# Gathers of a paged latent cache spread over the tiles in which their memory is free, and pooling sums moved ahead of the rotations

## The chip, the cores and the metric

One Trainium2 chip, of which the kernel uses one core. The metric is the device time of one execution in microseconds (us). The kernel before took 2307.67 us, the median of 3 runs (2307.08 to 2310.55).

## The reference, cut to what matters

One layer of a decoder runs over two kinds of input: a prompt of 1024 tokens, and 8 decode sequences with one new token each and 8192 cached tokens each. All arithmetic is float32. The parts the change touches are these.

```python
# pooling: trailing means over 2, 4, 8, 16 positions minus the token, one window per channel group
win = end[..., ch] - cs[:, P + 1 - w:P + 1 - w + S, ch]
diffs.append(win / cnt - bf[:, P:, ch])
# latents and the shared rotary key
ckv = rms_norm(c_kv_raw, g_kv_a);  kpe = apply_rope(k_pe_raw, cos, sin)
# decode attention: for each of 8 sequences, over its 64 pages of 128 cached tokens
k = mla_keys(cache_ckv[phys], cache_kpe[phys], w_uk, g_kn)     # keys from the latent, RMS-normed per head
s = einsum('bqhd,bkhd->bhqk', q, k) * scale                    # then softmax over 8192 tokens
acc = acc * alpha + einsum('bhqk,bkc->bhqc', p, ckv_blk)       # weighted latents
```

`cache_ckv` holds 256 floats for each cached token and `cache_kpe` 32. `page_table` says which physical page is which.

## The kernel before, in words

The program has four stages: input projection with the per-head projections behind it (about 0 to 248 us), prompt attention (to 418 us), decode attention over the cache (419 to about 1400 us), and the output projection with the gated MLP. Every engine has its own instruction stream, written out by hand, and waits on semaphores. The order of the text of a stream is its order of execution.

**Decode attention** (`cache_and_merge`). The 8 sequences (b = 0 to 7) follow one another. Each has 64 tiles of 128 tokens, handled as 32 pairs (n = 0 to 31), and 8 chunks of 8 tiles. For each pair TensorE transposes two tiles of the following pair into PSUM (`turn`, L1676), then makes keys of this pair with 12 matmuls (`keys`, L1700). ScalarE copies the transposed latents to SBUF (`hi`, L1872), VectorE makes their low part (L2063), ScalarE squares the keys (L1972), and VectorE takes the scores (L2176, semaphore `scored`) and the sums of squares (L2178, semaphore `summed`, one increment per tile). `summed` therefore counts tiles that are done. Every fourth pair also handles the rotary keys of a chunk (L1708, L1716). Ahead of pair 18 of sequence b+1, that is once its tile 36 is the next, TensorE makes the softmax-weighted latents of sequence b (`weigh`, L1728, 130 matmuls, semaphore `weighted`). From then on the latents of sequence b are dead. VectorE and ScalarE also build the key weights of the following sequence in pairs 17 to 25 of sequences 0 to 6 (L2030, L2038, L1977).

**Gathers** (`gather`, L1401). The latents come by indirect DMA, issued from GpSimd's stream. One chunk is two transfers: 128 KB of rotary keys into a ring of 12 slots, and 1 MB of latents into `lat[par][n]`, where par is the sequence's parity. So there are 16 transfers per sequence and two sequences' memory. Chunk 0 of sequence 0 is gathered at the start of the prompt attention. When the cache stage begins, GpSimd issues chunks 1 to 7 of sequence 0 without a wait, then `paced(1)`. After that, for each b, it runs `tail(b)` (norms and scaled scores of sequence b), waits for `weighted` of b, and issues `paced(b + 2)`. `paced(b)` issues chunk 0 at once and chunk n when `summed` has reached 7n tiles of sequence b-1. As `weighted` comes at tile 36, the conditions 7, 14, 21, 28 and 35 are already met for b of 2 and more: chunks 0 to 5 go out back to back, chunk 6 at tile 42, chunk 7 at tile 49. For b = 1 nothing has to be weighed first, so the eight chunks go out at tiles 0, 7, 14 and so on.

**Input projection** (`inputs_and_heads`). Nine tiles are projected by TensorE; the order is the decode tokens first and then the eight prompt tiles. GpSimd's stream has two duties for each tile n. `rotate(n)` (L550 to L555) rotates the shared key of tile n once VectorE has copied it (`kpe_out`, L503); its result (`roped`) lets VectorE copy the next. `average(n - 2)` (L575 to L590) makes the pooling sums of prompt tile n-2 once ScalarE has stored that tile (`u_kept`, L316), and it also contains the subtraction for the tile before (`subtract`, L596, semaphore `averaged`). The loop does `rotate(n)`, then `average(n - 2)`. After the loop come `average(7)`, `subtract(7)`, and then the rotations of the query heads (`heads.gpsimd`, L1035 to L1040, semaphore `rotated`). In the head stage behind it, ScalarE's copy of the values of tile 1 (L868) waits until `averaged` has reached 8, since its destination lies in the memory around the pooling input; TensorE's transposes (L783) need the PSUM banks that ScalarE empties, and those of the query heads need `rotated`.

Of the kernel before, what the change touches and what calls it, by code (L numbers as in the profile page):

```python
# [124 lines left out]
def inputs_and_heads(nc, io, keep):  # L125
# [9 lines left out]
    with ExitStack() as stack:  # L135
# [397 lines left out]
        def _(pool):  # L533
# [11 lines left out]
            def rotate(n):  # L545
                pool.wait_ge(kpe_out, n + 1)
                a, b_ = kpe_raw[:, 0:HR], kpe_raw[:, HR:DR]
                i = ORDER[n]
                cos, sin = keep.cos[:, i, :], keep.sin[:, i, :]
                nc.gpsimd.tensor_tensor(rot[:, 0, :], a, cos, ALU.mult)  # L550
                nc.gpsimd.tensor_tensor(rot[:, 1, :], b_, sin, ALU.mult)
                nc.gpsimd.tensor_tensor(rot[:, 2, :], b_, cos, ALU.mult)
                step(nc.gpsimd.tensor_tensor(rot[:, 3, :], a, sin, ALU.mult))
                step(nc.gpsimd.tensor_tensor(keep.kpe[:, i, 0:HR], rot[:, 0, :], rot[:, 1, :], ALU.subtract))
                nc.gpsimd.tensor_tensor(keep.kpe[:, i, HR:DR], rot[:, 2, :], rot[:, 3, :], ALU.add).then_inc(roped, 1)  # L555
# [14 lines left out]
            def average(i):  # L570

                c0, add = HIST + i * P, ALU.add
                uT = keep.uT
                pool.wait_ge(u_kept, i + 2)
                step(nc.gpsimd.tensor_tensor(sum2[:], uT[:, :, c0 - 14:c0 + P], uT[:, :, c0 - 15:c0 + P - 1], add))  # L575
                if i >= 1:
                    subtract(i - 1)
                step(nc.gpsimd.tensor_tensor(sum4[:], sum2[:, 1:4, 2:142], sum2[:, 1:4, 0:140], add))
                step(nc.gpsimd.tensor_tensor(sum8, sum4[:, 1:3, 4:140], sum4[:, 1:3, 0:136], add))
                step(nc.gpsimd.tensor_tensor(sum16[:], sum8[:, 1, 8:136], sum8[:, 1, 0:128], add))  # L580
                if i >= 1:
                    pool.wait_ge(averaged, i)
                sums = (sum2[:, 0, 14:142], sum4[:, 0, 12:140], sum8[:, 0, 8:136], sum16[:])
                for g, src in enumerate(sums):
                    last = nc.gpsimd.tensor_scalar(mean[:, g, :], src, 1.0 / WINDOWS[g], 1.0, ALU.mult, ALU.mult)
                step(last)
                if i == 0:
                    pool.wait_ge(counts_in, 16)
                    for g, src in enumerate(sums):
                        last = nc.gpsimd.tensor_tensor(mean[:, g, 0:16], src[:, 0:16], keep.counts[:, g, :], ALU.mult)  # L590
                    step(last)

            def subtract(i):

                tile = keep.uT[:, :, HIST + i * P:HIST + (i + 1) * P]
                nc.gpsimd.tensor_tensor(tile, mean, tile, ALU.subtract).then_inc(averaged, 1)  # L596

            pool.wait_ge(w_lo_done, DC)
            for n in range(2, NT):
                rotate(n)  # L600
                average(n - 2)
            average(PT - 1)
            subtract(PT - 1)
            pool.wait_ge(pages_in, 16 * 12)
# [771 lines left out]
CHUNKS = PAST // CHUNK  # L1376
TILES = PAST // P
# [25 lines left out]

def cache_and_merge(nc, io, keep):

    PACE = 7
    with ExitStack() as stack:
        c = Ctx(nc, stack, "ca")
        slot_in = keep.slot_in
# [77 lines left out]
        keyed, squared, summed, scored = c.sem("keyed"), c.sem("squared"), c.sem("summed"), c.sem("scored")  # L1487
# [112 lines left out]
        @block.gpsimd  # L1600
        def _(pool):
            def chunk_sums(i):

                n = width(i)
                pool.wait_ge(mix_squared, i + 1)
                step(nc.gpsimd.tensor_tensor(msq[:, :, 0:2, 0:n], msq[:, :, 0:2, 0:n], msq[:, :, 2:4, 0:n], ALU.add))
                nc.gpsimd.tensor_tensor(msq[:, :, 0, 0:n], msq[:, :, 0, 0:n], msq[:, :, 1, 0:n], ALU.add)\
                  .then_inc(chunks_added, 1)

            def tail(b):  # L1610

                par = b % 2
                if b >= 1:
                    pool.wait_ge(shifted, b)
                for n, (a, z) in enumerate(PARTS if b == NB - 1 else ((0, TILES),)):
                    if n == 1:
                        chunk_sums(0)
                    pool.wait_ge(summed, b * TILES + z)
                    pool.wait_ge(pe_summed, b * CHUNKS + z // 8)
                    step(nc.gpsimd.tensor_tensor(mean[:, a:z], ss[:, par, a:z], kss[:, par, a:z].unsqueeze(2)  # L1620
                                                 .to_broadcast([P, z - a, NH]), ALU.add))
                    nc.gpsimd.tensor_scalar(mean[:, a:z], mean[:, a:z], 1.0 / DH, EPS, ALU.mult, ALU.add)\
                      .then_inc(averaged, 1)
                    pool.wait_ge(scored, b * TILES + z)
                    pool.wait_ge(pe_out, b * CHUNKS + z // 8)
                    step(nc.gpsimd.tensor_tensor(raw[:, par, a:z], raw[:, par, a:z], rot[:, par, a:z], ALU.add))
                    pool.wait_ge(averaged, b + 1 + n)
                    pool.wait_ge(guessed, b + 1 + n)
                    step(newton_rsqrt(nc.gpsimd, step, guess[:, a:z], mean[:, a:z], guess[:, a:z], tmp[:, a:z]))
                    step(nc.gpsimd.tensor_tensor(raw[:, par, a:z], raw[:, par, a:z], guess[:, a:z], ALU.mult))  # L1630

                nc.gpsimd.tensor_copy(raw[:, par, TILES, :], keep.s_new[:, b, :]).then_inc(complete, 1)
                if b == NB - 1:
                    chunk_sums(1)

                pool.wait_ge(reduced, b + 1)
                nc.gpsimd.tensor_tensor(raw[:, par], raw[:, par], top_all[:].unsqueeze(1)
                                        .to_broadcast([P, TILES + 1, NH]), ALU.subtract).then_inc(shifted, 1)

            step = Steps(pool, pool_step)  # L1640

            def paced(b):

                for n in range(CHUNKS):
                    if n >= 1:
                        pool.wait_ge(summed, (b - 1) * TILES + PACE * n)
                    gather(nc, io, keep, b, (n,))

            gather(nc, io, keep, 0, range(1, CHUNKS))
            pool.wait_ge(keep.mixed_stored, 16 * (1 + NH // 2))  # L1650
            paced(1)
            for b in range(NB):
                tail(b)
                if b + 2 < NB:
                    pool.wait_ge(weighted, b + 1)
                    paced(b + 2)
            for i in range(2, NT):
                chunk_sums(i)
            down.gpsimd(pool)
# [1172 lines left out]
```

## Time and profile before

| | |
|---|---|
| median of 3 runs | 2307.67 us |
| profiled execution, own time | 2308.59 us |
| its span (first to last instruction) | 2306.8 us |
| TensorE busy | 2208.0 us, 96% of the span |
| VectorE busy | 1420.0 us, 62% |
| ScalarE busy | 957.0 us, 41% |
| GpSimd busy | 362.3 us, 16% |
| software DMA queue (GpSimd's) | 84.92 MB, 10.1% of the engines' time |

A view by windows gives for each stretch of the execution how long every engine was busy (in the order PE, PEld, DVE, ACT, POOL, with the count of instructions), the granted TensorE clock (1.00 is 2.4 GHz, 0.50 is 1.2 GHz), the share of the 16 DMA engines' time that was used, and GB/s. The chain of waits goes back from the last instruction to what released it. In a timeline, the bracket at the end of a row says how long the engine had been idle before the instruction and what ended that.

### The profile page before, as it was taken

How to read it: one execution, taken by the hardware profiler on the slowest of the kernel's cores; microseconds unless marked ns; L12 is line 12 of the kernel's file. 1: busy time of each engine (PE TensorE's matmuls, PEld its weight loads, DVE VectorE, ACT ScalarE, POOL GpSimd, SP SyncE). 2: the span in 40 equal slices, each digit the busy share in tenths (PEclk: the TensorE clock that was granted, in tenths of full speed). 3: DMA queues.
4: the chain of work that ended last, by engine and by line, in shares of the span. 5: the costliest groups of instructions: out<-in, count | busy, mean ns of one | idle time of the engine just before them, and what ended most of it. 6: DMA issues, size and time to landing. Idle time of an engine off the chain costs nothing.

```text
span 2306.8 us, 34165 instructions
## 1 busy us (share of the span) xinstructions
PE 2208.0 (96%) x12929; PEld 1856.8 (80%) x12929; DVE 1420.0 (62%) x2682; ACT 957.0 (41%) x1829; POOL 362.3 (16%) x501
## 2 busy tenths in 40 slices
PE   8989899799999999999898999999999999999999
PEld 7977566688687877778686877879999999988776
DVE  4346676476565666667565766666767676754345
ACT  4445565355454545445454554321211111133334
POOL 2454111311212212031212103200000000000000
PEclk9999999999999999999999999999999999999999
DMA  5300100520312203040404013321111111143443
GB/s 166 63 18 1 58 16 19 201 101 26 133 37 86 84 30 136 6 165 6 165 5 172 12 42 127 116 79 46 45 45 45 45 45 45 36 148 118 165 170 132
DMA packets 94627, 182.17 MB, mean 79 GB/s; under 512 B 9264, under 2 KB 64384, under 8 KB 86127
## 3 DMA queue, kind: packets, MB, share of 16 engines
q1 hardware_dynamic: 78781, 95.48, 12.7%
q0 software_dynamic: 15712, 84.92, 10.1%
q8 instruction: 82, 1.34, 0.2%
q14 instruction: 52, 0.43, 0.1%
HBM read 166.34 MB, written 14.35 MB: 78 GB/s over the span
## 4 chain that ended last, share of the span: by engine, by line
PE 77%; issue 2%; DVE 1%; ACT 1%; another core or an unknown queue 1%; DMA 0%; POOL 0%; SPq 0%; DVEq 0%; ACTq 0%; POOLq 0%
PE ca_banks L1700 31%; PE ca_banks L2334 21%; PE ca_banks L2607 10%; PE ca_banks L1676 5%; PE ca_banks L1781 4%; PE ca_banks L1728 3%; PE ca_banks L1716 1%; PE ca_banks L1708 1%; PE ca_banks L2583 0%; PE ca_banks L1812 0%; DVE ca_room L2445 0%; DMA ca_x<-in_x_prompt 0%; DVE ca_down_lo L2647 0%; PE ca_banks L1765 0%
## 5 line engine op out<-in xcount | busy, mean ns | idle before, releaser
L1700 PE MATMUL ca_banks<-cache_w_hi,ca_hi 128*128 128x512 f32 x1024 | 431.1, 421 | 46.0 <-DVE ca_cells L2176 24.1
L1972 ACT ACTIVATE ca_banks<-ca_banks 128x512 f32<-128x512 f32 x512 | 297.9, 582 | 390.6 <-PE ca_banks L1700 247.1
L1700 PE MATMUL ca_banks<-cache_w_lo,ca_hi 128*128 128x512 f32 x1024 | 406.1, 397 | 0.0
L1700 PE MATMUL ca_banks<-cache_w_hi,ca_lo 128*128 128x512 f32 x1024 | 405.8, 396 | 0.0
L2178 DVE TENSOR_REDUCE ca_cells<-ca_banks 128x8 f32<-128x512 f32 x512 | 348.3, 680 | 0.0
L1700 PEld LDWEIGHTS ca_banks<-cache_w_hi,ca_hi 128*128 128x128 f32 x1024 | 195.8, 191 | 83.9 <-issue 47.5
L2063 DVE TENSOR_TENSOR ca_lo<-ca_banks,ca_hi 128x512 fp32r<-128x512 f32 x256 | 175.7, 686 | 103.9 <-ACT ca_hi L1872 82.7
L2176 DVE TENSOR_TENSOR ca_cells<-ca_banks,attn_coef 128x8 f32<-128x8 f32 x512 | 84.5, 165 | 243.3 <-ACT ca_banks L1972 228.7
L1700 PEld LDWEIGHTS ca_banks<-cache_w_hi,ca_lo 128*128 128x128 f32 x1024 | 195.5, 191 | 46.0
L1700 PEld LDWEIGHTS ca_banks<-cache_w_lo,ca_hi 128*128 128x128 f32 x1024 | 196.7, 192 | 32.8
L1872 ACT ACTIVATE ca_hi<-ca_banks 128x512 fp32r<-128x512 f32 x256 | 152.6, 596 | 92.5 <-PE ca_banks L1676 79.6
L2445 DVE RECIPROCAL ca_room<-ca_room 128x1032 f32<-128x1032 f32 x22 | 145.3, 6603 | 0.8
L2607 PE MATMUL ca_banks<-ca_down_hi,ca_g_hi 128*128 128x512 f32 x352 | 113.9, 405 | 2.1 <-DVE ca_gT L2448 1.9
L2379 ACT ACTIVATE ca_room<-ca_banks 128x1032 f32<-128x1032 f32 x22 | 22.8, 1035 | 219.9 <-PE ca_banks L2334 219.9
L2334 PE MATMUL ca_banks<-mlp_h_hi,ca_gate_hi 128*128 128x344 f32 x528 | 113.4, 321 | 0.6 <-DVE mlp_h_lo L2141 0.6
L2647 DVE TENSOR_TENSOR ca_down_lo<-ca_down_raw,ca_down_hi 128x1024 fp32r<-128x1024 f32 x44 | 53.9, 1225 | 97.1 <-ACT ca_down_hi L2638 97.1
L2334 PE MATMUL ca_banks<-mlp_h_lo,ca_gate_hi 128*128 128x344 f32 x528 | 113.3, 320 | 0.0
L2334 PE MATMUL ca_banks<-mlp_h_hi,ca_gate_lo 128*128 128x344 f32 x528 | 112.7, 319 | 0.0
L1401 POOL DMA_INDIRECT cache_kpe<-in_cache_kpe,attn_index x64 | 61.3, 958 | 326.1 <-DVE ca_cells L2178 152.1
L2334 PE MATMUL ca_banks<-mlp_h_hi,ca_up_hi 128*128 128x344 f32 x528 | 112.2, 321 | 0.0
L2334 PE MATMUL ca_banks<-mlp_h_lo,ca_up_hi 128*128 128x344 f32 x528 | 111.6, 319 | 0.0
L2334 PE MATMUL ca_banks<-mlp_h_hi,ca_up_lo 128*128 128x344 f32 x528 | 111.5, 319 | 0.0
(408 smaller groups left out, 4086.6 us busy)
## 6 DMA issues: line engine op xcount, KB each, us to landing
ca_down_raw<-in_w_down SPq DMA_DIRECT2D x44, 512.0 KB, 3.3
keep_w_uv<-in_w_gate SPq DMA_DIRECT2D x22, 512.0 KB, 3.8
ca_up_raw<-in_w_up SPq DMA_DIRECT2D x22, 512.0 KB, 3.6
keep_ctx<-in_w_down SPq DMA_DIRECT2D x22, 512.0 KB, 3.4
late_room<-in_x_prompt SPq DMA_DIRECT2D x8, 512.0 KB, 3.9
ca_m<-mixed_scratch SPq DMA_DIRECT2D x8, 512.0 KB, 4.3
ca_w_raw<-in_w_o SPq DMA_DIRECT2D x16, 256.0 KB, 2.5
ca_x<-in_x_prompt SPq DMA_DIRECT2D x8, 512.0 KB
```

Of the source, the lines that this page charges most:

```text
L1676: last = nc.tensor.transpose(TT[:, n % 2, (2 * t + ck) * P:(2 * t + ck + 1) * P], src, keep.ident[:])
L1700: last = nc.tensor.matmul(KK[:, t, :], x[:, n % 2, t, ck, :], w[:, par, ck, :], start=(m == 0), stop=(m == 5))
L1728: last = nc.tensor.matmul(CT[q * 32:q * 32 + NH, 0:RK], probs[:, t, :], v, start=(t < 4), stop=(t >= TILES - 3))
L1781: last = nc.tensor.matmul(OUT[0:n, a, g, :], h[:, k, 0:n], w[:, k, g * 512:(g + 1) * 512], start=(k == 4 * a and q == 0), stop=(k == 4 * a ...
L1872: nc.scalar.activation(hi[:, n % 2], TT[:, n % 2, :].rearrange("p (t c k) -> p t c k", t=2, c=2), ACT.Copy).then_inc(hi_done, 1)
L1972: nc.scalar.activation(SQ[:, t, :], KK[:, t, :], ACT.Square).then_inc(squared, 1)
L2063: nc.vector.tensor_tensor(lo[:, n % 2], TT[:, n % 2, :].rearrange("p (t c k) -> p t c k", t=2, c=2), hi[:, n % 2].bitcast(F32), ALU.subtra ...
L2176: nc.vector.tensor_tensor(raw[:, par, 2 * n + t, :], KK[:, t, :].rearrange("p (h d) -> p h d", d=DN)[:, :, 0], keep.coef[:, b, :], ALU.mul ...
L2178: nc.vector.tensor_reduce(ss[:, par, 2 * n + t, :], SQ[:, t, :].rearrange("p (h d) -> p h d", d=DN), AX.X, ALU.add).then_inc(summed, 1)
L2334: ins = nc.tensor.matmul(GU[kind][:, j, :], w[kind][:, k, :], h[:, k, j * F3:(j + 1) * F3], start=(k == 0 and n == 0), stop=(k == DC - 1 a ...
L2445: link(nc.vector.reciprocal(sig, sig))
L2607: last = nc.tensor.matmul(self.OUT[t][:, h, :], g[b][:, t * P:(t + 1) * P], w[b][:, h * 512:(h + 1) * 512], start=(f == 0 and k == 0), sto ...
```

## The change

Four edits. The loop of the input projection does `average(n - 2)` before `rotate(n)`. `paced(b)` issues chunk n, chunk 0 included, when `summed` has reached 36 + 7n // 2 tiles of sequence b-1, which is 36, 39, 43, 46, 50, 53, 57 and 60. Chunks 1 and 2 of sequence 0 go out at once and chunk n from 3 to 7 when `summed` has reached 8(n - 2), which is 8, 16, 24, 32 and 40. `paced(1)`, behind them, follows the same rule of 36 to 60. The number and size of the transfers, their destinations and all arithmetic are the same.

```diff
@@ inputs_and_heads, gpsimd
             pool.wait_ge(w_lo_done, DC)
             for n in range(2, NT):
+                average(n - 2)
                 rotate(n)
-                average(n - 2)
             average(PT - 1)
             subtract(PT - 1)
@@ cache_and_merge
-    PACE = 7
+    START, PACE = 36, 7
@@ cache_and_merge, gpsimd
                 for n in range(CHUNKS):
-                    if n >= 1:
-                        pool.wait_ge(summed, (b - 1) * TILES + PACE * n)
+                    pool.wait_ge(summed, (b - 1) * TILES + START + PACE * n // 2)
                     gather(nc, io, keep, b, (n,))
 
-            gather(nc, io, keep, 0, range(1, CHUNKS))
+            gather(nc, io, keep, 0, (1, 2))
+            for n in range(3, CHUNKS):
+                pool.wait_ge(summed, TILES // CHUNKS * (n - 2))
+                gather(nc, io, keep, 0, (n,))
             pool.wait_ge(keep.mixed_stored, 16 * (1 + NH // 2))
             paced(1)
```

## Rows read from the trace of the kernel before

**Rows 1.** The page: its first line, and the chain of waits by engine.

```profile
span 2306.8 us, 34165 instructions
...
PE 77%; issue 2%; DVE 1%; ACT 1%; another core or an unknown queue 1%; DMA 0%; POOL 0%; SPq 0%; DVEq 0%; ACTq 0%; POOLq 0%
```

**Rows 2.** Chain of waits in sequence 1 (start us, us, what).

```profile
621.00 4.21 another core or an unknown queue
```

**Rows 3.** Windows: stretch and its us, engines' busy us, PEclk, DMA share, GB/s.

```profile
430.99:447.10 16.11, 5.46 (x20) 4.23 (x19) 4.04 (x10) 2.87 (x6) 6.89 (x8) 0.68 0.94 386
457.15:460.58 3.43, 3.43 (x19) 2.86 (x18) 2.80 (x8) 1.69 (x4) 1.28 (x2) 1.00 0.00 0
620.49:631.55 11.06, 5.99 (x21) 4.41 (x20) 4.92 (x12) 3.02 (x6) 6.03 (x7) 0.69 1.00 404
743.91:754.77 10.86, 5.74 (x21) 4.20 (x20) 4.64 (x12) 3.00 (x6) 5.79 (x7) 0.69 1.01 406
867.28:877.87 10.59, 5.54 (x21) 4.05 (x20) 4.43 (x12) 3.00 (x6) 5.54 (x7) 0.84 1.01 408
990.23:1000.81 10.58, 5.49 (x22) 4.04 (x21) 4.39 (x11) 3.00 (x6) 5.55 (x7) 0.84 1.01 403
1113.27:1125.99 12.72, 6.17 (x21) 4.85 (x20) 5.19 (x12) 3.09 (x6) 5.93 (x7) 0.73 0.93 368
1238.35:1252.37 14.02, 6.10 (x21) 4.83 (x20) 5.10 (x12) 3.00 (x6) 5.95 (x7) 0.63 1.00 387
1364.88:1368.55 3.67, 3.67 (x21) 3.14 (x20) 3.47 (x9) 2.52 (x5) 0.00 (x0) 1.00 0.25 76
```

**Rows 4.** GpSimd's timeline: first and last gather of a burst, one paced gather.

```profile
610.90 1.02 POOL L1401 DMA_INDIRECT cache_kpe<-in_cache_kpe,attn_index  x1 [22.45 <-PE ca_banks L1728]
...
625.26 0.95 POOL L1401 DMA_INDIRECT cache_lat_late<-in_cache_ckv,attn_index  x1 [0.30 <-issue]
...
642.09 0.95 POOL L1401 DMA_INDIRECT cache_kpe<-in_cache_kpe,attn_index  x1 [10.16 <-DVE ca_cells L2178]
```

**Rows 5.** Windows of four pairs each in sequence 0: pairs 8 to 11, 20 to 23.

```profile
460.58:474.06 13.48, 13.48 (x72) 11.30 (x71) 9.15 (x22) 7.34 (x15) 2.49 (x3) 1.00 0.29 102
...
501.02:514.63 13.61, 13.61 (x72) 11.32 (x71) 10.63 (x26) 8.29 (x17) 1.89 (x2) 1.00 0.26 88
```

**Rows 6.** A window of the input projection.

```profile
54.00:60.00 6.00, 6.00 (x41) 5.61 (x39) 1.52 (x7) 3.11 (x7) 5.61 (x9) 1.00 0.98 180
```

**Rows 7.** GpSimd's timeline, end of the pooling sums.

```profile
165.50 1.14 POOL L575 TENSOR_TENSOR in_sum<-mid_uT 128x568 f32<-128x568 f32 x1
...
171.98 1.18 POOL L596 TENSOR_TENSOR mid_uT<-late_room,mid_uT 128x512 f32<-128x512 f32 x1
173.12 0.46 POOL L1035 TENSOR_TENSOR keep_ctx<-keep_ctx,late_cos 128x128 f32<-128x128 f32 x1
```

**Rows 8.** ScalarE's timeline, same stretch.

```profile
144.13 0.60 ACT L316 ACTIVATE mid_uT<-in_tr 128x512 f32<-128x512 f32 x1 [6.10 <-PE in_tr L399]
...
173.19 0.60 ACT L868 ACTIVATE mid_v<-in_tr 128x512 f32<-128x512 f32 x1 [8.58 <-POOL mid_uT L596]
...
176.09 0.20 ACT L856 ACTIVATE hd_log<-hd_mean 128x16 f32<-128x16 f32 x1
```

**Rows 9.** TensorE's timeline, same stretch.

```profile
173.84 1.09 PE L783 MATMUL in_tr<-keep_ident,hd_k_nat 128*96 128x128 f32 x4 [6.17 <-ACT mid_v L868]
175.91 1.91 PE L783 MATMUL in_tr<-keep_ident,keep_ctx 128*96 128x128 f32 x8 [0.98 <-POOL keep_ctx L1040]
```

**Rows 10.** VectorE's timeline: the last step of tile 1's mean.

```profile
173.22 0.39 DVE L963 TENSOR_SCALAR hd_mean<-hd_ss 128x16 f32<-128x16 f32 x1
```

**Rows 11.** GpSimd's timeline of one tile: rotation, then last pooling step.

```profile
95.15 0.22 POOL L550 TENSOR_TENSOR in_rot<-in_kpe_raw,late_cos 128x16 f32<-128x16 f32 x1 [7.77 <-DVE in_kpe_raw L503]
...
101.95 0.30 POOL L585 TENSOR_SCALAR late_room<-in_sum 128x128 f32<-128x128 f32 x1
```

**Rows 12.** ScalarE's timeline of the same tile.

```profile
87.19 0.58 ACT L316 ACTIVATE mid_uT<-in_tr 128x512 f32<-128x512 f32 x1
```

## The prediction, made before the changed kernel was run

> **What bounds the kernel now.** I read the page's chain of waits by engine first: 77% of it is TensorE [rows 1]. So a change counts only where it shortens TensorE's idle time, or lengthens it. The small shares beside it are the interesting ones: "issue" 2% and "another core or an unknown queue" 1% are waits for which the profile has no releaser. Following the chain in order of time through the decode attention, one such piece of 4 to 7 us stands in each of the sequences 0 to 6, as the 4.21 us at 621.00 [rows 2]. Nothing of the program's own ended it.
>
> Next I took the start of each pair's transposes from TensorE's timeline and asked the windows for the pairs in which these pieces lie [rows 3]. Pair 21 of sequence 7 takes 3.67 us, with no gather issued in it (GpSimd 0.00). Pair 21 of sequences 1 to 6 takes 11.06, 10.86, 10.59, 10.58, 12.72 and 14.02 us. In sequence 0 it is pair 3, with 16.11 us against 3.43 us for pair 7 of the same sequence. TensorE was busy for 5.5 to 6.2 us of each, the granted clock averages 0.63 to 0.84 (part of it at 1.2 GHz, after the idle time), and the DMA engines were in use 93 to 101% of the time at 368 to 408 GB/s. The same place in the program costs 7 to 13 us more exactly where a burst of gathers is in flight: in sequences 1 to 6 twelve transfers go out back to back, the first at 610.90 and the last at 625.26 [rows 4], 6.75 MB in all.
>
> In the input stage the same kind of reading finds one more hole: TensorE waits 6.17 us for ScalarE's L868 [rows 9], which had waited 8.58 us for GpSimd's last pooling subtraction [rows 8].
>
> **The change part by part.**
>
> *Gathers paced.* Excess of the seven pairs [rows 3]: 16.11 - 3.43 = 12.68, then minus 3.67 each: 7.39, 7.19, 6.92, 6.91, 9.05 and 10.35; the sum is 60.49 us. This includes the half clock behind each hole. The pairs around them stand at their regular length, so nothing is hidden elsewhere. After the change no two chunks go out closer than 3 tiles, except chunks 1 and 2 of sequence 0. A pair takes 13.48 / 4 = 3.37 us [rows 5], so 3.5 tiles are 5.9 us. A chunk is 1.125 MB, 2.9 us at 404 GB/s: one chunk is landed 3 us before the next is issued. Whether that is sparse enough is answered by gathers that are paced already: seven chunks of sequence 1, 7 tiles apart, go out during sequence 0, and chunk 7 of each later one goes out alone, as at 642.09 [rows 4]. Four pairs that contain one or two of them last 13.48 and 13.61 us [rows 5]. So an isolated chunk costs 0 to 0.13 us. There are 63 chunks behind the first, so 0 to 8 us. I take 0, the value of the first row, since the 13.61 also holds the building of the next weights. Upper bound of the loss from the opening of sequence 0, where four transfers still go back to back: its 12.68 us stay. Lower bound: 0. I take 0: an issue of the burst takes (625.26 - 610.90) / 11 = 1.31 us, so the hole at 621.00 comes after some eight transfers, four chunks, not two.
>
> What queues behind the new waits: on GpSimd, `paced(1)` waits behind chunk 7 of sequence 0, and `tail(b)` behind the last gather. The last gather is now issued at tile 60 (it was tile 49) and takes two issues of 0.95 us [rows 4], about 1.1 tiles with the gaps; `tail` itself waits for tile 64. Cost 0, cover about 3 tiles, 5 us. Who needs the data: chunk n of sequence 0 is issued at tile 8(n - 2) and transposed from tile 8n - 2, 14 tiles or 24 us later; for the other sequences chunk 0 has 26 tiles and chunk 7 has 58. Cost 0. The waits for the ring of rotary keys are met earlier than the new conditions.
>
> *Sums ahead of rotations, at the end.* After the last rotation GpSimd now has one set of sums left, not two. One set takes 171.98 - 165.50 = 6.48 us there [rows 7]; tile 6's own is ready from 144.13 + 0.60 [rows 8] and runs before the rotation. So `averaged` reaches 8 at about 166.7 instead of 173.16, L868 runs 6.5 us earlier and the head rotations start 6.4 us earlier; TensorE's transposes at 173.84 and 175.91 [rows 9] move with them. A smaller wait comes into view: VectorE ends tile 1's mean at 173.61 [rows 10] and ScalarE's logarithm of it ran at 176.09 [rows 8], so that chain gains only 2.5 us. It gates the transposes of the next tile, which come behind a whole projection, and I take that as slack enough. Without the 6 us of idle time the clock should also stay up behind it; I put 0.5 us on that, an estimate. I take 7 us; bounds 0 (the chain of VectorE and ScalarE holds everything) and 8.6 (ScalarE's whole idle time).
>
> *Sums ahead of rotations, in the loop.* A rotation now waits behind a set of sums. For one tile: the input is stored at 87.19 + 0.58 = 87.77 [rows 12], the sums take 102.25 - 96.47 = 5.8 us (the rotation at 95.15 takes 1.3 and the last step ends at 102.25) [rows 11], so they end at 93.6, 1.6 us before the rotation can start. Cost 0 with 1.6 us of cover. With the cover gone VectorE copies the next key late, and TensorE needs that PSUM bank only one tile later. The sums now run beside VectorE's normalisation; some of those small instructions may wait for GpSimd. Bounds -1 to +5 us over seven tiles; I take 0.
>
> *Sum.* 2308.59 - 60.49 - 7 = 2241.1 us for an execution like the profiled one. That one lies 0.92 us over the median of the runs, so 2240.2 us; I write 2240.
>
> **A rule against this.** TensorE's holes coincide with a saturated DMA in [rows 3]. The Trainium skill, page "SBUF — State Buffer", section "Who interferes with whom", says that a DMA never contends with a compute engine and that PE and ACT never wait on anyone. By that rule the transfers do not cause the holes, pacing changes nothing, and the sum would be about 2301. No row shows a hole with the DMA engines idle, so the trace does not agree so far.
>
> **Rivals.**
>
> *The holes are not the burst's.* Their place is always pair 21 in sequences 1 to 6, where the next key weights are made (pairs 17 to 25), and sequence 7, without a hole, makes none. Also, 6 us of fully used DMA in the input stage leave TensorE 6.00 of 6.00 us busy [rows 6]. Then only the pooling part counts: 2307.67 - 7 = 2300.7. Against it: pairs 20 to 23 of sequence 0 make those weights with only single chunks in flight and take 13.61 us for all four [rows 5], and the hole of sequence 0 is at pair 3, where no weights are made. The rule above would do the same here. Chance 6%.
>
> *Part of the hole stays.* If it comes with a certain number of transfers close together, sequence 0's opening can keep its 12.7: 2253. If each of the seven keeps half, 30 us, 2270. For it: the hole starts 10 us after the first issue, well inside the burst, and ends while the burst goes on, so it is not the length of the burst that sets it. Against it: the paced chunks show nothing of it. Chance 12% and 8%.
>
> *Slower: one hole for each stretch of transfers.* Each burst has exactly one hole, though it keeps the DMA full for 17 us. If the hole belongs to the beginning of a stretch that meets a bad moment, there are now 8 stretches a sequence where there were two. At two holes of 6.9 us a sequence, 2 x 6.91 x 7 = 96.7 us come for 60.5: 2307.67 + 36.2 - 7 = 2337. It decides from ten holes on (67.5 / 6.91 = 9.8) in about 56 stretches. Against it: 13 single chunks in the trace without one. Chance 3%.
>
> **How the numbers follow.** All holes gone 71%, opening of sequence 0 kept 12%, halves kept 8%, no effect 6%, slower 3%. The range goes from 2235 (60.5 + 8.6 off the median, and the runs' own spread of 3) to 2266 (opening kept, isolated chunks at 0.13 us each, no gain in pooling: 2307.67 - 47.8 + 8 = 2268). A difference below 0.2%, 4.6 us, can't be told from none. Faster by more 96%; the same 1%; slower 3%.
>
> **What would show it.** Right: no pair in the decode attention over 4 us outside the weighings; seven unattributed pieces gone from the chain; the granted clock at 1.00 from 420 to 1340 us; gathers of later sequences 5 to 7 us apart; L868 about 6.5 us earlier, and TensorE's first matmul of the cache stage at about 412 instead of 419. Wrong: holes at pair 21 with the DMA engines half idle (first rival), shorter holes (second), more than one a sequence (third), or rotations that end later than before in the loop.

## The result, and the profile after

| | before | after |
|---|---|---|
| median | 2308.07 us (4 runs, 2307.08 to 2310.55) | 2243.4 us (4 runs, 2240.52 to 2243.67) |
| profiled execution, span | 2306.8 us | 2241.9 us |
| ratio after / before | | 0.9716, 95% interval 0.9701 to 0.9732 |

That is 64.7 us less; 67.5 was forecast, and 2240. But one of the four chips of the experiments below ran the kernel before in 2248.8 us, and there the pacing brought nothing. So the larger part of this gain depends on the chip, or on its state at the time. The excess of TensorE's time at a burst of gathers is called a hole from here on.

The page after: engines, and the chain of waits by engine.

```profile
PE 2191.6 (98%) x12929; PEld 1845.9 (82%) x12929; DVE 1425.7 (64%) x2682; ACT 955.5 (43%) x1829; POOL 363.4 (16%) x501
PE 79%; DVE 1%; ACT 1%; issue 0%; DMA 0%; POOL 0%; ACTq 0%; DVEq 0%; POOLq 0%
```

"issue" went from 2% to 0% and "another core or an unknown queue" from 1% to nothing [rows 1]. The windows after for the places of [rows 3] (stretch and its us, engines' busy us, PEclk, DMA share, GB/s): pair 3 of sequence 0, pair 21 of sequences 1 and 6, and two neighbouring pairs late in sequence 0.

```profile
424.18:427.61 3.43, 3.43 (x20) 2.86 (x19) 2.79 (x8) 1.69 (x4) 0.00 (x0) 1.00 0.00 0
602.88:606.66 3.78, 3.78 (x22) 3.16 (x20) 3.78 (x11) 1.92 (x4) 0.00 (x0) 1.00 0.85 277
...
1183.72:1187.52 3.80, 3.80 (x21) 3.17 (x20) 3.80 (x11) 1.91 (x4) 0.00 (x0) 1.00 0.83 276
495.13:499.75 4.62, 3.73 (x19) 2.60 (x17) 2.16 (x6) 2.73 (x6) 0.82 (x1) 1.00 0.97 379
499.75:503.89 4.14, 3.86 (x21) 3.16 (x20) 3.36 (x9) 1.91 (x4) 1.57 (x2) 1.00 0.50 195
```

Pair 3 went from 16.11 to 3.43 us, and pair 21 of the six sequences from 10.6 to 14.0 to between 3.75 and 3.80. The last two rows are new: pairs 24 and 25 of sequence 0, whose like (every fourth pair, by the starts of the transposes) take 3.20 and 3.67 us elsewhere, take 4.62 and 4.14. GpSimd's timeline of that place shows why (start us, us, what; two rows of ten).

```profile
483.15 0.94 POOL L1401 DMA_INDIRECT cache_kpe<-in_cache_kpe,attn_index  x1 [11.29 <-DVE ca_cells L2180]
...
495.00 0.94 POOL L1401 DMA_INDIRECT cache_lat_far<-in_cache_ckv,attn_index  x1 [0.30 <-issue]
```

Ten transfers went out back to back. `paced(1)` stands behind chunk 7 of sequence 0, which waits for tile 40. By then its own conditions 36 and 39 are met, and 43 and 46 are met while it catches up.

The cache stage as a whole, first of before, then of after:

```profile
419.25:1396.31 977.06, 930.64 (x5384) 754.23 (x5385) 629.86 (x1500) 495.39 (x940) 202.51 (x206) 0.98 0.22 83
```

```profile
412.43:1331.41 918.98, 916.84 (x5383) 745.41 (x5384) 628.57 (x1500) 493.92 (x940) 200.88 (x206) 1.00 0.27 88
```

It is 58.08 us shorter; the other 6.8 of the span's 64.9 us come before it. The head stage after, by engine:

```profile
166.67 1.18 POOL L596 TENSOR_TENSOR mid_uT<-late_room,mid_uT 128x512 f32<-128x512 f32 x1
167.81 0.64 POOL L1035 TENSOR_TENSOR keep_ctx<-keep_ctx,late_cos 128x128 f32<-128x128 f32 x1
168.41 1.04 POOL L1036 TENSOR_TENSOR keep_ctx<-keep_ctx,late_sin 128x128 f32<-128x128 f32 x1
167.89 0.60 ACT L868 ACTIVATE mid_v<-in_tr 128x512 f32<-128x512 f32 x1 [2.10 <-POOL mid_uT L596]
172.66 0.22 ACT L856 ACTIVATE hd_log<-hd_mean 128x16 f32<-128x16 f32 x1 [2.03 <-DVE hd_mean L963]
168.28 1.05 PE L783 MATMUL in_tr<-keep_ident,hd_k_nat 128*96 128x128 f32 x8 [1.50 <-DVE hd_k_nat L988]
171.42 1.91 PE L783 MATMUL in_tr<-keep_ident,keep_ctx 128*96 128x128 f32 x8 [2.09 <-POOL keep_ctx L1040]
```

ScalarE's L868 waits 2.10 us instead of 8.58 [rows 8], and TensorE's hole of 6.17 us before the key transposes [rows 9] is 1.50 us, ended by VectorE. The query transposes now wait 2.09 us for GpSimd's rotation.

### The profile page after: what moved, and what is told of

It reads as the page before. It is cut to its first block, busy times and chain, and to the rows that moved or that the text cites. A ratio compares the mean times of both kernels' runs of the same rounds, so it can differ in the third digit from the quotient of the medians.

```text
span 2241.9 us, 34172 instructions
## 1 busy us (share of the span) xinstructions
PE 2191.6 (98%) x12929; PEld 1845.9 (82%) x12929; DVE 1425.7 (64%) x2682; ACT 955.5 (43%) x1829; POOL 363.4 (16%) x501
## 4 chain that ended last, share of the span: by engine, by line
PE 79%; DVE 1%; ACT 1%; issue 0%; DMA 0%; POOL 0%; ACTq 0%; DVEq 0%; POOLq 0%
PE ca_banks L1702 31%; PE ca_banks L2336 22%; PE ca_banks L2609 11%; PE ca_banks L1678 5%; PE ca_banks L1783 4%; PE ca_banks L1730 3%; PE ca_banks L1718 1%; PE ca_banks L1710 1%; PE ca_banks L2585 0%; PE ca_banks L1814 0%; DVE ca_room L2447 0%; DVE ca_down_lo L2649 0%; DMA ca_w_raw<-in_w_o 0%; ACT ca_down_hi L2640 0%; PE ca_banks L1767 0%
## 5 line engine op out<-in xcount | busy, mean ns | idle before, releaser
L1702 PE MATMUL ca_banks<-cache_w_hi,ca_hi 128*128 128x512 f32 x1024 | 424.7, 415 | 1.7 <-DVE ca_cells L2178 1.1
L1702 PE MATMUL ca_banks<-cache_w_lo,ca_hi 128*128 128x512 f32 x1024 | 401.2, 392 | 0.0
```

Of the source, the lines that this page charges most:

```text
L1702: last = nc.tensor.matmul(KK[:, t, :], x[:, n % 2, t, ck, :], w[:, par, ck, :], start=(m == 0), stop=(m == 5))
```

## The experiments

The experiments were timed on four chips, with the kernel before beside them on each. On three it took 2305.7 to 2312.5 us, on one 2248.8; the three are called chips with holes. The first result (2308.07 us before) is of such a chip too; which one is not on record. Each of the four was seen in one stretch of runs only, so the chip itself and its state at that time are not told apart. The diffs below are cut to the lines that matter; `...` marks what is left out.

**sums_only: the first edit alone.**

```diff
             for n in range(2, NT):
+                average(n - 2)
                 rotate(n)
-                average(n - 2)
```

> The kernel before with the first edit alone: in the input loop and nowhere else, the pooling sums stand ahead of the rotation. My theory: the holes of the decode attention stay (seven, 60.5 us in all), the head stage gains 5.1 us at the transposes behind ScalarE's copy of the values and the loop loses 1.2 us, since VectorE's normalisation runs beside GpSimd's sums; net -3.9 us by the end of the heads. In the trace of the changed kernel another 2.9 us came in the prompt attention, where no edit lies. If that belongs to the edit it comes again here: 2307.7 - 6.8 = 2300.9, first matmul of the cache stage at about 412.4. Rival: it is an accident of where the clock falls, and the total is -3.9: 2303.8, first matmul at about 415.3. A second rival, from the prediction: the edit loses more in the loop than it gains, 2308 to 2312.

**later_only: the pacing of `paced(b)` alone.**

```diff
-    PACE = 7
+    START, PACE = 36, 7
...
-                    if n >= 1:
-                        pool.wait_ge(summed, (b - 1) * TILES + PACE * n)
+                    pool.wait_ge(summed, (b - 1) * TILES + START + PACE * n // 2)
```

> The kernel before with the pacing of paced(b) alone (tiles 36, 39, 43, 46, 50, 53, 57, 60 of the sequence before); the chunks 1 to 7 of sequence 0 still go out back to back, and the pooling is as before. Burst theory: the six holes of sequences 1 to 6 go, 47.8 us; the opening of sequence 0 is now 14 transfers, not 18 in 19 us, since paced(1) waits for tile 36, and keeps a hole of about 10 to 12 us at pair 3. 2307.7 - 47.8 = 2260, or 2258 if the shorter burst has a shorter hole. Rival (the holes belong to the place where the next key weights are made, not to the burst): nothing changes, 2308.

**first_only: the opening of sequence 0 alone.**

```diff
-            gather(nc, io, keep, 0, range(1, CHUNKS))
+            gather(nc, io, keep, 0, (1, 2))
+            for n in range(3, CHUNKS):
+                pool.wait_ge(summed, TILES // CHUNKS * (n - 2))
+                gather(nc, io, keep, 0, (n,))
```

> The kernel before with the opening of sequence 0 alone changed: chunks 1 and 2 at once, chunks 3 to 7 at tiles 8 to 40; paced(b) as before. paced(1) is then behind a wait for tile 40, so that its conditions 0, 7, 14, 21, 28 and 35 are all met when it starts: chunk 7 of sequence 0 and chunks 0 to 5 of sequence 1 go out back to back at tile 40 of sequence 0, 14 transfers. Burst theory: the hole of sequence 0 is not removed but moves from pair 3 to pairs 24 to 26, 7 to 11 us long; total 2307.7 - 12.7 + 9.5 = 2304.5 (2303 to 2307). Rival (the opening of the stage is what makes the hole of sequence 0, or pair 21 the others): the hole at pair 3 goes and none comes, 2307.7 - 12.7 = 2295.

These three, and the first run of `bursts`, shared one chip, where the kernel before took 2248.78 us (21 runs, 2244.91 to 2251.48). Measured: sums_only 2240.54, ratio 0.996 (0.9947 to 0.9974); later_only 2248.7, ratio 0.9997 (0.9988 to 1.0006); first_only 2246.24, ratio 0.9987 (0.9977 to 0.9997). All three forecasts of the total missed. In later_only and first_only both theories missed, since there was nothing to remove. The pooling edit brought 8.2 us (5.8 to 11.9 by the interval), more than the 3.9 or 6.8 expected; the part on why the prediction came out right comes back to it. Windows of sums_only and first_only around the burst of sequence 1, which is as the kernel before has it:

```profile
591.12:618.18 27.06, 27.06 (x144) 22.03 (x137) 19.23 (x48) 15.06 (x29) 15.18 (x16) 1.00 0.80 310
```

```profile
596.98:624.03 27.05, 27.05 (x144) 22.05 (x137) 19.23 (x48) 15.06 (x29) 15.18 (x16) 1.00 0.80 310
```

Sixteen transfers in 27 us, the DMA in use 80% of it, and TensorE busy all the time. This is also the regular length of the stretch, some 140 matmuls, in which all bursts below are compared.

**bursts: bursts of chosen length** (sequence 0's chunks 3 to 7 at tiles 6 to 30).

```diff
+    BURST = (0, 3, 2, 4, 5, 6, 7, 8)
...
-                    pool.wait_ge(summed, (b - 1) * TILES + START + PACE * n // 2)
+                    pool.wait_ge(summed, (b - 1) * TILES + START + (PACE * n // 2 if n >= BURST[b] else 0))
```

> The changed kernel with bursts of chosen length. Sequence 0's chunks 3 to 7 at tiles 6, 12, 18, 24 and 30; then for b = 1 to 7 the first 3, 2, 4, 5, 6, 7 and 8 chunks back to back when tile 36 of the sequence before is done, the rest at the changed kernel's tiles. Nothing else differs. Burst theory: the hole opens 10 us after the first issue, which is 8 transfers, and lasts about until the last issue. So 2, 3 and 4 chunks (4, 6, 8 transfers, up to 10 us) leave no hole; 5 chunks 2 to 4 us of excess; 6 chunks 7 to 10; 7 chunks 9 to 11; 8 chunks 11 to 13. Together about 34 us: 2243 - 2 + 34 = 2275. Rival 1 (one hole per stretch of transfers, of one length): each burst of three chunks and more has about 7 us, six of them, 2285. Rival 2 (the hole has a fixed length and belongs to the tenth transfer): 5, 6, 7 and 8 chunks have 7 us each, 2270.

2242.82 us and no hole, not even for eight chunks. The same burst of 8 chunks in its window:

```profile
1170.64:1197.62 26.98, 26.98 (x144) 22.07 (x137) 19.23 (x48) 15.05 (x29) 15.26 (x16) 1.00 0.87 340
```

**after_again: the changed kernel, on another chip.**

> The changed kernel once more, beside the kernel before on the chip of this job. The three single edits showed that the kernel before takes 2248.8 us, not 2308, on the chip of that job, and has no hole in any burst, also of 16 transfers. So the holes belong to a chip (or its state) and the burst together. If this job's chip has none: the pacing is worth 0, the pooling 6 to 8 us, 2241 against 2249. If it has them as the first did: 2243 against 2308.

2240.66 us (5 runs) against 2307.04 of the kernel before (9 runs), ratio 0.9725 (0.9704 to 0.9747): a chip with holes, and the first result again. All experiments below but last_sum_six are single runs, as `bursts` was.

**last_sum_six: two alterations for the two losses seen.**

```diff
             for n in range(2, NT):
-                average(n - 2)
+                if n == NT - 1:
+                    average(n - 2)
                 rotate(n)
+                if n < NT - 1:
+                    average(n - 2)
...
-                pool.wait_ge(summed, TILES // CHUNKS * (n - 2))
+                pool.wait_ge(summed, 6 * (n - 2))
```

> The changed kernel with two alterations: only the last rotation (tile 8) stands behind the sums, the others ahead of them as before; and sequence 0's chunks 3 to 7 go out at tiles 6, 12, 18, 24 and 30, so that paced(1) starts at its own tile 36 and does not catch up. My account of the changed kernel's trace: the loop of the input stage gets back the 1.2 us that VectorE lost beside GpSimd's sums, on any chip; the catch-up of ten transfers at 483 us cost 1.9 us on the first chip and nothing where there are no holes. So -1.2 against after_again on a chip without holes, -3.1 on one with. Rival: the 1.2 us at 62 us was an accident of the arrival of the tile (the input landed later), and nothing is gained; or the next-to-last sum then ends later and the gain in the head stage shrinks, up to +6.

On the same chip as after_again: 2242.38 us, ratio to before 0.9727 (0.9709 to 0.9744), no different from 0.9725, where 3.1 us less had been expected. In the traces the two losses did go. The loop of the input stage took 23.23 us instead of after_again's 23.75. Here are windows of after_again and then of last_sum_six over the same instructions, the entry of the cache stage and the catch-up:

```profile
401.14:423.25 22.11, 18.90 (x145) 15.86 (x146) 9.96 (x26) 10.39 (x23) 3.91 (x4) 1.00 0.39 143
472.15:501.20 29.05, 27.82 (x143) 22.59 (x142) 20.23 (x49) 15.54 (x31) 11.87 (x12) 1.00 0.56 216
```

```profile
400.91:426.11 25.20, 21.99 (x146) 18.48 (x147) 9.97 (x26) 10.52 (x23) 4.14 (x5) 0.86 0.34 126
475.00:502.10 27.10, 27.10 (x143) 22.61 (x142) 20.32 (x49) 15.65 (x31) 9.31 (x10) 1.00 0.52 178
```

The catch-up's 1.95 us are gone (29.05 to 27.10), but in this profile the entry of the stage ran in part at 1.2 GHz (0.86) and took 3.09 us more. No edit accounts for that: TensorE's work is the same, and the chunk that goes out earlier does so at the end of the window.

**kinds: seven bursts of different kinds.** b is the sequence whose cache is gathered, which happens during sequence b - 1. Of b = 3 the twelve transfers are plain ones on SyncE's queue; of b = 2 the latents are left out.

```diff
+    SIX = (36, 36, 36, 36, 36, 36, 57, 60)
+    AT = {1: SIX, 2: SIX, 3: SIX, 4: (48, 48, 48, 48, 48, 48, 60, 63), 5: (36, 38, 40, 42, 44, 46, 57, 60),
+          6: (36, 36, 36, 44, 44, 44, 57, 60), 7: SIX}
...
+            if name == "cache_ckv" and b == 2 and n < 6:
+                name, dst = "cache_kpe", dst[:, 0:8 * DR]
...
+                            sp.dma_start(dst, rows[P * n:P * n + P, :]).then_inc(plain_in[n], 16)
```

> The kernel last_sum_six's opening of sequence 0 with the changed kernel's pooling, and in sequences 0 to 6 six kinds of burst for the chunks 0 to 5 of the next one. Seq 0 and seq 1's kinds start when tile 36 is done. Sequence 0: six chunks back to back (control). Sequence 1: the same 12 transfers with an eighth of the bytes (the latents are replaced by the rotary keys' rows, which leaves out the latents). Sequence 2: the same bytes and destinations by plain transfers on SyncE's hardware queue (consecutive pages, which leaves out the paging). Sequence 3: the six chunks at tile 48. Sequence 4: one chunk for every 2 tiles, 3.4 us, from tile 36. Sequence 5: three chunks at tile 36, three at 44. Sequence 6: control again. Where the chip has the holes (its kernel before takes about 2307), the theory 'a long stretch of saturated DMA slows TensorE, wherever it comes' expects: controls 7 to 10 us of excess; small ones 0; hardware queue 7 to 10; tile 48: 7 to 10, six pairs later, so the building of weights has no part; 2 tiles: 0 to 2; three and three: 0. Rival 1 (GpSimd's software queue fills up with transfers): small ones 7 to 10 as well, hardware queue 0. Rival 2 (the place: it needs the building of weights beside the transfers): tile 48 gives 0 or much less. Where the chip has none (before about 2249): all zero.

2275.06 us, on a chip with holes (before 2312.52). Windows of some 140 matmuls, regularly 27.0 to 27.1 us: control, latents' transfers with an eighth of their bytes (2/9 of the burst's), hardware queue, tile 48, one chunk per 2 tiles, three and three, control.

```profile
476.67:511.58 34.91, 29.19 (x143) 23.84 (x141) 20.41 (x49) 15.75 (x31) 11.58 (x12) 0.95 0.53 204
599.67:634.59 34.92, 29.92 (x145) 23.73 (x137) 19.42 (x48) 15.28 (x29) 11.90 (x12) 0.90 0.16 46
723.73:750.72 26.99, 26.99 (x144) 22.03 (x137) 19.24 (x48) 15.06 (x29) 0.00 (x0) 1.00 0.66 263
861.36:896.19 34.83, 29.87 (x143) 24.15 (x142) 18.81 (x45) 14.70 (x29) 13.44 (x15) 0.90 0.60 230
963.99:990.97 26.98, 26.98 (x145) 22.04 (x137) 19.24 (x48) 15.06 (x29) 11.93 (x12) 1.00 0.75 263
1080.19:1109.15 28.96, 27.36 (x144) 22.06 (x137) 19.12 (x48) 15.32 (x29) 11.46 (x12) 1.00 0.66 246
1198.29:1232.62 34.33, 29.20 (x145) 23.26 (x138) 19.43 (x48) 15.28 (x29) 11.96 (x12) 0.90 0.58 222
```

Excess over the regular length: 7.8, 7.9, 0, 7.8, 0, 1.9, 7.3 us. Read the second row against the third: with the DMA in use 16% of the time the hole is there in full, and with 66% on the other queue there is none. The theory of the saturated DMA falls, and so does the place (row 4: the hole moved with the burst, and the usual place in that sequence, without a burst, took 27.06 us). Rival 1 of the expectation, GpSimd's software queue, came out as it said; `counts` below tests it further. Three and three cost 1.9 us, where the theory had 0.

**bursts_again: the lengths, on that chip.** The kernel is that of `bursts`.

> The kernel of bursts of 3, 2, 4, 5, 6, 7 and 8 chunks in sequences 0 to 6, again, on another job's chip. On the chip of its first run it had no hole at all, nor had the kernel before. Where the chip has the holes, burst theory as before: 2, 3 and 4 chunks nothing, 5 chunks 2 to 4 us of excess, 6 chunks 7 to 10, 7 chunks 9 to 11, 8 chunks 11 to 13, about 34 us in all, 2275. One hole of fixed length per long stretch: 7 us each for 5, 6, 7 and 8 chunks. Where the chip has none: 2241 to 2243 as in its first run.

2287.34 us, where 2275 was expected: the holes add up to 42.1 us, not 34, and the rest of the difference is not accounted for. Sequences 0 to 6, with bursts of 3, 2, 4, 5, 6, 7 and 8 chunks:

```profile
477.24:505.46 28.22, 27.14 (x143) 22.61 (x142) 20.41 (x49) 15.63 (x31) 9.29 (x10) 1.00 0.47 171
593.54:620.58 27.04, 27.04 (x144) 22.03 (x137) 19.24 (x48) 15.05 (x29) 8.58 (x9) 1.00 0.51 176
709.72:739.13 29.41, 27.08 (x145) 22.03 (x138) 19.33 (x48) 15.26 (x29) 8.60 (x9) 1.00 0.43 161
828.34:862.45 34.11, 29.12 (x145) 23.45 (x138) 19.42 (x48) 15.26 (x29) 10.00 (x10) 0.90 0.45 173
951.59:987.86 36.27, 29.71 (x145) 24.02 (x137) 19.51 (x48) 15.35 (x29) 11.44 (x12) 0.86 0.51 196
1077.08:1113.87 36.79, 30.45 (x145) 24.14 (x138) 19.52 (x48) 15.35 (x29) 13.82 (x14) 0.86 0.58 225
1203.01:1242.38 39.37, 28.70 (x145) 22.75 (x137) 19.23 (x48) 15.26 (x29) 15.40 (x16) 0.87 0.64 254
```

Excess 1.1, 0, 2.4, 7.1, 9.3, 9.8, 12.4 us. It grows with the burst and has no fixed length. Each is one burst in one run; twelve transfers cost 7.3 to 9.3 us in the five plain windows of kinds, bursts_again and counts. My rule "hole from the eighth transfer" was off: six transfers already cost 1.1 us. The step from 2.4 to 7.1 is where the clock falls too (0.90).

**counts: what in a transfer counts.** (Twelve transfers each unless said otherwise; "few" rows leave the others out.)

```diff
...
+            if b == 5 and n < 6:
+                nc.gpsimd.dma_start(dst, rows[P * n:P * n + P, :]).then_inc(keep.slot_in[s], 16)
+                continue
+            few = {3: 64, 6: 16}.get(b, P) if n < 6 else P
...
+            nc.gpsimd.indirect_dma_start(dst[0:few], None, rows, at).then_inc(keep.slot_in[s], 16)
...
+                        for i, name in enumerate(("cache_kpe", "cache_ckv")):
+                            pool.wait_ge(summed, (b - 1) * TILES + 36 + 2 * n + i)
```

> Seven more kinds of the burst of chunks 0 to 5, one in each sequence 0 to 6, from tile 36. On the last chip with holes, 6 transfers cost 1.1 us, 8 cost 2.4, 10 cost 7.0, 12 cost 7.3 to 9.3, an eighth of the bytes cost the same 7.8, and the same bytes on SyncE's hardware queue nothing. So it is GpSimd's side of the software queue. Sequence 0: control. Sequence 1: the six latents transfers alone back to back (1 MB each), the rotary keys later, one per tile from tile 50. Sequence 2: 12 transfers that gather 64 of the 128 rows (the other half is left out). Sequence 3: 12 single transfers, one per tile, 1.69 us apart instead of 1.25. Sequence 4: 12 plain transfers from GpSimd (software queue, no indices, consecutive pages, which leaves out the paging). Sequence 5: 12 transfers of 16 rows. Sequence 6: control. Theory 'each transfer from the software queue past about the fifth in a row delays TensorE by about 1 us, whatever it holds': latents alone 1 us, 64 rows and 16 rows 7 to 9 as the control, one per tile 0 to 4, plain 7 to 9. Theory 'it is the number of descriptors that GpSimd writes in a short time': 64 rows about 1 to 2.4 us, 16 rows 0, plain ones by their packets. Theory 'it is the indices': plain 0, the others 7 to 9. On a chip without holes all are zero.

2283.17 us, on a chip with holes (before 2305.69). Control, six latents alone, 64 rows, one transfer per tile, plain from GpSimd, 16 rows, control:

```profile
474.32:509.22 34.90, 29.25 (x143) 23.78 (x142) 20.42 (x49) 15.74 (x31) 11.32 (x12) 0.95 0.53 204
597.30:624.91 27.61, 27.16 (x144) 22.03 (x137) 19.23 (x48) 15.26 (x29) 6.64 (x7) 1.00 0.59 229
714.06:751.66 37.60, 29.78 (x144) 24.05 (x137) 19.41 (x48) 15.26 (x29) 10.87 (x12) 0.86 0.45 95
840.88:867.90 27.02, 27.02 (x145) 22.02 (x137) 19.27 (x48) 15.05 (x29) 11.40 (x12) 1.00 0.73 263
957.04:984.03 26.99, 26.99 (x145) 22.03 (x138) 19.24 (x48) 15.05 (x29) 6.50 (x12) 1.00 0.66 263
1073.24:1111.02 37.78, 29.26 (x145) 23.29 (x137) 19.42 (x48) 15.16 (x29) 10.36 (x12) 0.91 0.08 24
1200.16:1235.62 35.46, 30.71 (x145) 24.54 (x137) 19.41 (x48) 15.16 (x29) 11.41 (x12) 0.86 0.56 215
```

Excess 7.8, 0.6, 10.6, 0, 0, 10.8, 8.5 us. Sixteen rows, a DMA share of 0.08, and the largest hole of the table: neither the rows nor the bytes count. Plain transfers from the same engine and queue cost nothing, though they go out faster, one per 0.54 us. What remains is the count of *indirect* transfers of GpSimd close together: twelve of them 1.25 us apart cost, twelve at one per tile not (in the trace 1.84 us apart in the mean, 1.25 to 3.4, so the 1.69 of the expectation is a mean too). None of the three theories fits all seven rows as written. "It is the indices" gets the plain row right and misses two (six alone 0.6 us, one per tile 0); the first gets those two right and misses the plain row. Both together, a count that only indirect transfers add to, fit all seven but for size: 10.6 and 10.8 us where 7 to 9 was expected. Two things stay untested. The rate is not separated from the count within some 10 us. And the plain transfers also read consecutive pages, so indices and scattered addresses are not told apart; indirect transfers of consecutive pages would do it.

**later_again: later_only on that chip.**

> The kernel before with the pacing of paced(b) alone, again. On the chip without holes it took the time of before (2248.7 against 2248.8). On one with holes: the six holes of sequences 1 to 6 go, and sequence 0 keeps one for its 14 transfers back to back; by the bursts of known length that costs 9.7 us (14 transfers) where the 16 of before cost 12.7. Before 2308 - 47.1 - 3.0 = 2258. Rival, that the opening's hole is of another kind and stays at 12.7: 2261.

2261.37 us, 44.3 less than that chip's 2305.69. The opening's 14 transfers cost 11.8 us over the regular progress of TensorE's matmuls, between my 9.7 and the rival's 12.7, nearer the rival. By the theory 47.8 us go in sequences 1 to 6 and 0.9 in the opening; 44.3 is 4 short of that, but these are single runs, and those of the kernel before spread from 2302.2 to 2311.4 on another such chip. The trace itself shows no hole outside the opening: TensorE is busy for all of 541 to 1100 us at a granted clock of 1.00. So on a chip with holes the pacing of `paced(b)` alone removes six of them and leaves the one of sequence 0, and the changed kernel, which paces the opening too, has none there (3.43 us for pair 3 above).

## Why the prediction came out right, and where it did not

- *The holes belong to the burst of gathers.* Right in place and size on chips with holes: 60.5 us forecast, 58.1 measured in the stage. The reason I leaned on beside it, the full DMA engines, is refuted by `kinds` and `counts`. The forecast did not need it, since pacing takes away both; that the wrong reason did no harm was luck.
- *"No two chunks go out closer than 3 tiles, except chunks 1 and 2 of sequence 0."* This step failed. I had written that `paced(1)` queues behind chunk 7, and did not ask which of its conditions would be met by then. The sign that I had named for being right, no pair over 4 us, is broken there. Ten transfers in a row cost 1.9 us (29.05 against 27.10). And 3.67 us was the wrong base for pair 21: where the next weights are made it takes 3.80, as in sequence 0 of the kernel before (504.22 to 508.03, 3.81) and, with no gather in flight, in sequence 3 of kinds (850.62 to 854.41, 3.79). That is 0.1 us six times, and the two make up about the 2.4 us by which the stage falls short.
- *The opening of sequence 0 costs nothing, since holes begin after some eight transfers.* Right in value: the four transfers at 413 us cost nothing, like the two chunks of `bursts_again`. As a count it was off: six transfers cost 1.1 us there, and six latents alone 0.6 in `counts`.
- *The sums at the end: 7 us.* TensorE's stretch around it, first before, then after, then last_sum_six:

```profile
164.28:180.93 16.65, 8.05 (x34) 6.21 (x33) 12.71 (x25) 4.32 (x9) 13.15 (x24) 0.69 0.00 0
```

```profile
165.45:176.99 11.54, 7.95 (x33) 6.54 (x32) 10.55 (x25) 4.21 (x9) 7.43 (x14) 0.70 0.00 0
```

```profile
164.93:175.45 10.52, 6.91 (x34) 5.70 (x32) 9.57 (x25) 4.22 (x9) 6.41 (x13) 0.84 0.00 0
```

  It gained 5.1 us here and 6.1 in last_sum_six. The difference is not that kernel's edit: after_again, the same program as after, took 10.70 us at the same clock of 0.84, and gained 5.95. The last subtraction started 5.3 us earlier (166.67 against 171.98) although the work ahead of it ran 1.2 us later, which is the 6.5 us forecast. But the rotations behind it took longer (L1036 1.04 us instead of 0.46), so the query transposes moved by only 4.5 us (171.42 against 175.91), or 5.7 in the order of work. And part of the stretch still ran at half clock (0.70 or 0.84). Seven was 1 to 2 us too much.
- *The sums in the loop: 0, bounds -1 to 5.* Mis-sized. VectorE's normalisation of a tile, in after and then in last_sum_six, where the rotation is still first:

```profile
60.44 0.98 DVE L122 TENSOR_TENSOR in_rx<-in_lnx,in_gx 128x1 f32<-128x1 f32 x1
61.46 1.46 DVE L474 TENSOR_SCALAR late_room<-late_room,in_rx 128x1024 f32<-128x1024 f32 x1
```

```profile
60.38 0.16 DVE L122 TENSOR_TENSOR in_rx<-in_lnx,in_gx 128x1 f32<-128x1 f32 x1
60.57 0.75 DVE L474 TENSOR_SCALAR late_room<-late_room,in_rx 128x1024 f32<-128x1024 f32 x1
```

  L122 took 0.98 instead of 0.16 us and ended at 61.42, with GpSimd's L575 (60.28 and 1.13 us long), and L474 took 1.46 instead of 0.75 beside GpSimd's next two. The Trainium skill, page "SBUF — State Buffer", section "Who interferes with whom", says that VectorE and GpSimd share a port pair that one of them holds for a whole instruction; L122 agrees. TensorE waited for L474 once in after:

```profile
62.98 0.66 PE L378 MATMUL in_tr<-keep_ident,late_room 128*128 128x128 f32 x4 [0.66 <-DVE late_room L474]
```

  Over these matmuls, first before and then after, it lost 1.0 us:

```profile
59.52:82.76 23.24, 23.21 (x139) 21.32 (x138) 9.16 (x32) 10.33 (x29) 8.55 (x26) 1.00 0.41 66
```

```profile
59.63:83.90 24.27, 23.43 (x139) 21.27 (x138) 13.18 (x34) 11.01 (x31) 13.67 (x34) 1.00 0.45 69
```

  The tile was also ready some 0.6 us later in after (L470 at 59.68 instead of 59.00), which adds to the wait. The six profiles with this edit took 23.74 to 24.74 us here, so the loss is 0.5 to 1.5; last_sum_six, where the rotation is first but for the last tile, took 23.23.

- *A gain that I had not worked out.* 2.96 us of the prompt attention's 115.73 went, though no edit lies there. The same stretch of instructions in sums_only, whose program is that of after up to this point, took 115.93, in after_again 112.78, in last_sum_six 111.68, at granted clocks of 0.94, 0.97 and 0.98. So one program can do either, by where its half-clock stretches fall. That the total came so near was luck in this respect: without these 2.96 us the forecast of 7 for the pooling would have met 3.9. The profile of after is also the lowest of its kind: from the loop to the prompt attention (59.52 to 293.03 before) it gained 4.0 us, the five others with the edit 4.1 to 6.1. Whether the 2.96 us are chance alone is open. The profiled execution of sums_only, without them, was the slowest of its five (2244.36 us at a mean granted clock of 0.992); the other four took 2239.77 to 2241.39 at 0.994 to 0.995, while 20 of the 21 of the kernel before on that chip stood at 0.991 or 0.992. So the edit seems to make the better placing more frequent, which would explain its 8.2 us; no trace shows it.
- *The rule against this* is that of the Trainium skill, page "SBUF — State Buffer", section "Who interferes with whom": a DMA never contends with a compute engine, and TensorE never waits on anyone. As to bytes these runs agree: 263 GB/s on the hardware queue cost TensorE nothing. For GpSimd's indirect transfers the runs on three of the four chips disagree, and there the measurement decides. On the fourth, pacing changed nothing (ratio 0.9997), as the rule would have it.

The range held on chips with holes. Its upper end was written as 2266 where its own sum gives 2268, and the pieces of "4 to 7 us" in the chain are 3.85 us in sequence 4 and two in sequence 0 (4.90 and 6.39); nothing hung on either. On the fourth chip the prediction would have been wrong by nearly all of its first term, and nothing in the profile before could have told: every run behind it came from a chip with holes.

## What to carry to other kernels

Before a gain is put down to a kernel, time before and after on more than one chip: here the same change is worth 2.8% on chips with holes, and its single edits 0.4% (pooling), 0.1% (opening) and nothing (pacing) on one without. If indirect transfers of GpSimd go out in a burst beside TensorE's work, try spreading them: two per 3.4 us or one per tile, some 1.8 us, cost nothing here, while plain transfers, on either queue, cost nothing in a burst. And when a paced sequence starts behind another wait, check which of its conditions are met when it gets its turn: it catches up in one burst.

## What was not expected of the hardware

The chip matters: 2248.8 us against 2305.7 to 2312.5 for one program. Bursts of GpSimd's indirect transfers stalled TensorE's work on three of the four, and not on the fourth.

The stall shows as late signals before it shows as a gap. TensorE's transposes and ScalarE's copy that waits for them, kernel before, sequence 1:

```profile
617.28 0.60 PE L1676 MATMUL ca_banks<-keep_ident,cache_lat_far 128*128 128x128 f32 x4
```

```profile
620.97 0.60 ACT L1872 ACTIVATE ca_hi<-ca_banks 128x512 fp32r<-128x512 f32 x1 [1.64 <-DMA in_w_raw<-in_w_in]
```

The transposes are recorded as over at 617.9, ScalarE was free at 619.3, and its copy ran at 620.97. In the program that copy waits only for TensorE: for these transposes, and for keys whose last matmul is recorded ahead of them. So "DMA" as its releaser is a wrong guess of the view. TensorE's completions, or its signals, were late, while its records (whose ends the view models) still kept their even distances. Which of the two it is, what an indirect transfer takes from TensorE, and why one chip was spared, stays open.
